# The last four products of a diffusion block's second MLP, and the final norm, in parts of 384 and 128 tokens instead of 256 and 256

## The reference

```python
def rms_norm(x, g, eps=NORM_EPS):
    y = xf * lax.rsqrt(jnp.mean(xf * xf, axis=-1, keepdims=True) + eps)
    return (y * g.astype(jnp.float32)).astype(x.dtype)

def squared_relu_mlp(h, w_in, w_out):
    return jnp.square(jax.nn.relu(h @ w_in)) @ w_out
...
        xl = xl + ml[5] * squared_relu_mlp(modulate(xl, norm_mlp_g[i], ml[3], ml[4]), w_mlp_in[i], w_mlp_out[i])
...
    return rms_norm(xl, final_norm_g)
```

## Time and profile before

| | before |
|---|---|
| median of 3 runs | 1615.22 us (1614.89 to 1615.65) |
| the profiled execution's own time | 1615.17 us |
| its span in the trace | 1613.4 us |
| TensorE busy (matmuls) | 1593.0 us, 99% |
| TensorE weight loads | 1432.4 us, 89% |
| VectorE, ScalarE, GpSimd busy | 983.9, 517.4, 617.5 us |
| first matmul of the last four units | 1578.87 us |
| last store issued | 1611.12 us |

### The profile page before, as it was taken

The page is one execution under the profiler, slowest core; times in us unless marked ns, Lnnn a source line. Parts: engine busy times, 40 slices in busy tenths (PEclk is TensorE's granted clock), DMA queues, the critical chain, the costliest instruction groups (busy, mean ns, idle before and its releaser), DMA issues.

```text
span 1613.4 us, 24201 instructions
## 1 busy us (share of the span) xinstructions
PE 1593.0 (99%) x9427; PEld 1432.4 (89%) x9427; DVE 983.9 (61%) x1316; ACT 517.4 (32%) x931; POOL 617.5 (38%) x402
## 2 busy tenths in 40 slices
PE   8999999999999999999999999999999999999997
PEld 5889988989999999999999888878889888888887
DVE  5697457258756764864784678229975825344354
ACT  4422466333211211211211512138864422222222
POOL 2422565335323322432331444244504644444441
PEclk9999999999999999999999999999999999999999
DMA  9473212213252234223332122110002322323221
GB/s 357 185 278 140 92 41 100 92 66 105 76 186 79 78 120 141 98 97 117 105 111 98 66 91 92 66 56 1 1 1 89 105 95 92 104 91 100 95 79 53
DMA packets 50334, 162.99 MB, mean 101 GB/s; under 512 B 6336, under 2 KB 8768, under 8 KB 46656
## 3 DMA queue, kind: packets, MB, share of 16 engines
q1 hardware_dynamic: 50240, 161.68, 28.8%
HBM read 158.78 MB, written 2.10 MB: 100 GB/s over the span
## 4 chain that ended last, share of the span: by engine, by line
PE 93%; DVE 2%; DMA 2%; issue 1%; ACT 1%; SPq 0%; POOL 0%; POOLq 0%; DVEq 0%; ACTq 0%
PE ps L1713 27%; PE ps L1714 26%; PE ps L1715 26%; PE ps L2239 3%; PE ps L2201 2%; PE ps L2228 1%; PE ps L2106 1%; PE ps L2094 1%; PE ps L2134 1%; PE ps L1918 1%; DMA mod_big<-w_mod_dram 1%; DMA mod_late<-w_mod_dram 1%; DMA raw<-units_dram 1%; PE ps L2129 1%; DVE h L1315 0%
## 5 line engine op out<-in xcount | busy, mean ns | idle before, releaser
L625 POOL TENSOR_TENSOR w_lo<-raw,w_hi 128x1024 fp32r<-128x1024 f32 (+1 forms) x235 | 483.3, 2068 | 838.3 <-ACT w_hi L784 838.1
L1713 PE MATMUL ps<-h,w_hi 128*128 128x384 f32 (+2 forms) x1176 | 409.8, 348 | 1.8 <-DVE h L1315 1.4
L1714 PE MATMUL ps<-h,w_lo 128*128 128x384 f32 (+2 forms) x1176 | 407.6, 347 | 0.0
L1715 PE MATMUL ps<-h,w_hi 128*128 128x384 f32 (+2 forms) x1176 | 407.3, 346 | 0.0
L784 ACT ACTIVATE w_hi<-raw 128x1024 fp32r<-128x1024 f32 x187 | 197.8, 1058 | 373.5 <-PE ps L1715 366.0
L1713 PE MATMUL ps<-hid_lo,w_hi 128*128 128x384 f32 (+2 forms) x800 | 277.6, 347 | 0.0
L1714 PE MATMUL ps<-hid_hi,w_lo 128*128 128x384 f32 (+2 forms) x800 | 276.5, 346 | 0.0
L1715 PE MATMUL ps<-hid_hi,w_hi 128*128 128x384 f32 (+2 forms) x800 | 276.4, 346 | 0.0
L1713 PEld LDWEIGHTS ps<-h,w_hi 128*128 128x128 f32 x1176 | 221.3, 188 | 25.3 <-issue 3.4
L1715 PEld LDWEIGHTS ps<-h,w_hi 128*128 128x128 f32 x1176 | 221.2, 188 | 16.4
L1714 PEld LDWEIGHTS ps<-h,w_lo 128*128 128x128 f32 x1176 | 221.3, 188 | 16.0
(11 more groups left out here) (233 smaller groups left out, 2264.5 us busy)
## 6 DMA issues: line engine op xcount, KB each, us to landing
raw<-units_dram SPq DMA_DIRECT2D x187, 512.0 KB, 3.3
mod_ring<-w_mod_dram SPq DMA_DIRECT2D x96, 256.0 KB, 3.3
mod_big<-w_mod_dram SPq DMA_DIRECT2D x16, 1024.0 KB, 10.6
mod_late<-w_mod_dram SPq DMA_DIRECT2D x8, 1024.0 KB, 8.0
xl<-x_dram SPq DMA_DIRECT2D x2, 2048.0 KB, 8.4
bias<-bias_dram SPq DMA_DIRECT2D x8, 384.0 KB, 3.8
xc<-ctx_dram SPq DMA_DIRECT2D x2, 1024.0 KB, 10.4
out_dram<-out_t SPq DMA_DIRECT2D x16, 128.0 KB, 1.9
```

The source lines that it names most:

```text
L625: ins = nc.gpsimd.tensor_tensor(w_lo[:, s, sl], raw[:, s, sl], w_hi[:, s, sl].bitcast(F32), op=ALU.subtract)
L1713: mm(out, a[0], b[1], start=start, stop=False)
L1714: mm(out, a[1], b[0], start=False, stop=False)
L1715: return mm(out, a[0], b[0], start=False, stop=stop)
```

## The change

The final norm and the four units ahead of it (i = 4) are cut at token 384 instead of 256; the norm behind the second attention (i = 3) is still cut at 256. All that follows from a part's width follows: additions, squares, sums, diagonals, spreads, results and stores.

```diff
-        rows_last = at("rows_last", [P, 256], F32, a_at)
-        x_gain = at("x_gain", [P, 3, 256], F32, a_at + size(256))
+        rows_last = at("rows_last", [P, P], F32, a_at)
+        x_gain = at("x_gain", [P, 3, P], F32, a_at + size(256))
...
+        LAST = 384
...
-            half = slice(256 * j, 256 * j + 256)
+            edge = 256 if i == 3 else LAST
+            half = slice(edge, LAT) if j else slice(0, edge)
             return xl, 0, half, half
...
-                sp.dma_start(t["out"][:, k, 0:256], out_t[:, k, 0:256]).then_inc(out_stored, 16)
+                sp.dma_start(t["out"][:, k, 0:LAST], out_t[:, k, 0:LAST]).then_inc(out_stored, 16)
...
-                sp.dma_start(t["out"][:, k, 256:LAT], out_t[:, k, 256:LAT]).then_inc(out_stored, 16)
+                sp.dma_start(t["out"][:, k, LAST:LAT], out_t[:, k, LAST:LAT]).then_inc(out_stored, 16)
...
-                nc.gpsimd.tensor_tensor(out_t[:, k, 256:LAT], x_gain[:, k - 5], rows_last[:], op=ALU.mult).then_inc(out_pool, 1)
+                nc.gpsimd.tensor_tensor(out_t[:, k, LAST:LAT], x_gain[:, k - 5], rows_last[:], op=ALU.mult).then_inc(out_pool, 1)
...
-                        nc.scalar.activation(x_gain[:, m - 5], xl[:, m, 256:LAT], ACT.Copy,
+                        nc.scalar.activation(x_gain[:, m - 5], xl[:, m, LAST:LAT], ACT.Copy,
                                              scale=gains[:, 4, m:m + 1]).then_inc(gain_made, 1)
...
-                nc.scalar.activation(rows_last[:], ps[:, 7, 0:256], ACT.Copy).then_inc(rows_copied, 1)
+                nc.scalar.activation(rows_last[:], ps[:, 7, 0:P], ACT.Copy).then_inc(rows_copied, 1)
```

## The result

The changed kernel takes 1618.18 us (median of 17 runs, 1617.3 to 1619.89) against 1615.08 us for the kernel before in the same sets of runs: 3.1 us more, a ratio of 1.0020 with a 95% interval of 1.0014 to 1.0027. The forecast was 1618.8.

What follows compares the result with a forecast made beforehand. TensorE's stream was taken as the bound until 1602.9, then a 10.4 us tail. TensorE +4.72 (5.13 - 0.79 - 0.05 + 0.22 + 0.21) less 1.15 gave +3.6 us: 1618.8 us, range 1617.6 to 1620.1.

Steps and rivals of the forecast that it cites:

- The first pass's term: First pass of the last four units: 96 matmuls go from 256 to 384 columns, 119.9 to 173.3 ns each, +5.13 us.
- The second pass: Last four units: 96 matmuls go from 256 to 128 columns, 119.9 to 111.7 ns each, bound by weight loads, -0.79 us.
- The doubt about the repeated column: The 111.7 ns came from matmuls whose stationary operand repeats one column; full MLP tiles might load more slowly, staying at 119.9 ns.
- The rival in which the loads hide: Second pass runs at 60 ns a step with weight loads hidden: 4.96 us less, 1613.8 us, not slower; chance 4%.
- one pair of starts at a seam: Starts at 1197.64 and 1197.70, behind a 512-wide matmul: taken to show 128 columns alone need about 60 ns.
- VectorE's cover: Last units' second pass: VectorE free after about 2.6 us, next unit ready after 2.68; under 0.1 us spare, costed at 0.
- Sums and spread in the stream: On TensorE between units: a third sum matmul, +0.22 us, and a spread of 384 columns instead of 256, +0.21 us.
- The tail: Behind the last addition: narrower work brings the first store 1.08 us earlier, landing may give 0.1; about 1.15 us back.
- The landing: Landing of the last stores, 1.7 to 1.9 us: 64 KB instead of 128 may give -0.1 us.
- The steps on SyncE's queue: Seven further steps between the last eight stores, 3.30 us, some 0.48 each, set by the queue; taken to stay.
- the rival of faster stores: Half the bytes let SyncE's queue issue every 0.39 us: tail gives 0.57 us more, 1618.2 us; chance 17%.

## Why the prediction was right

*What bounds the kernel.* TensorE's stream from the first matmul of the last four units to the last addition grew by 4.76 us where 4.72 were summed, and the kernel by 3.4 in the trace. The first pass's term, +5.13, was measured alone as +5.1, with steps of 173.3 ns.

*The second pass.* 111.4 ns a step against 111.7 taken from another part of the kernel. The doubt about the repeated column in those rows was unneeded: full tiles load as fast. The rival in which the loads hide fell twice, in the changed profile and in the run with half the weights: a hidden load cannot shorten the step when it is halved, and this one did, to 60.0 ns. That run turned the argument from one pair of starts at a seam into a measurement. The argument itself had misread the pair: in the kernel before, too, the second narrow matmul's load starts with the first narrow matmul (both at 1197.64), so "about 60 ns" for the columns alone was an upper bound. Nothing in the sum hangs on it.

The price of this rival was wrong, 4.96 us less for 96 shorter steps. It left out VectorE's cover, which the prediction had itself found thin. In the run with steps of 60.0 ns VectorE held units 6 and 7, and the kernel gained 2.5; by that run the rival would have come to about 1615.7 (an estimate), not 1613.8.

The Trainium skill, "TensorE: Matmul & The Clock Gate", section Back-to-back issue gap, gives columns / 2.4 + 2.5 ns for an isolated matmul, and says itself that at few columns this leaves the weight load out. So the 111.4 ns measured here, where it has 55.8, do not contradict that section; the rule is not meant for such a stream.

*Sums and spread in the stream.* From the last matmul ahead of the sums (1597.95) to the second one behind them (1598.85) are 0.90 us, 0.68 above two plain steps, against 0.45 before (1593.14 to 1593.83): +0.23, with +0.22 summed. The spread's two sides are alike: 1601.31 to 1602.17, 0.64 above two steps against 0.44 before (1596.46 to 1597.14), +0.20 for a summed +0.21.

*VectorE's cover* was put at under 0.1 us. It held, and was wider. The three wide results of unit 6's turn in the changed kernel:

```profile
1605.88 1.66 DVE L1379 SCALAR_TENSOR_TENSOR out_t<-xl,gains,ps 128x384 f32<-128x384 f32 x3
```

They end at 1607.54, and the addition of unit 7 starts at 1607.62, 0.31 us behind the start of the unit's last matmul, as before (0.32): TensorE released it. The 0.08 between them is not the whole cover, since in the run with half the weight loads, where VectorE had no gap, the addition starts 0.09 ahead of the recorded end of the results. VectorE's period there was 2.50 us, against TensorE's 2.68, so the cover was some 0.18.

*The tail* gave 1.26 us where the terms add to 1.18 (the prediction wrote "about 1.15"). Two of its sizes were off, in opposite directions, so part of this closeness is luck. The final spread was summed as 0.49 and took 0.80 at a clock of 0.50, which made the first store 0.13 later than forecast. The landing was taken as 0.1 shorter; it went from 1.9 to 1.6 us, and the end followed 0.25 sooner; 1.6 us stayed with half the bytes. The steps on SyncE's queue stayed, as the sum took them and as two queues confirmed, so the rival of faster stores did not hold.

*The verdict.* The forecast of 3.6 us stands against 3.4 in the profiled pair and 3.1 between medians. The 0.3 between the last two is the profiled executions' own place among their runs, 0.41 above the median in the changed kernel and 0.09 in the one before. The prediction drew a line at 1618.45, 0.2% above before, and gave 0.72 to a time above it. The median of 1618.18 lies just below, on the side that had 0.25. But 0.2% was too coarse for what could be told: with 17 runs of each kernel the interval is 0.14% to 0.27%, and the changed kernel is slower.

## What to carry to other kernels

In this kernel a stream of matmuls that each load 128 new weight columns has a floor of one weight load a step, 111.4 ns. Splitting tokens unevenly across that floor costs on the wide side what the narrow side cannot give back, here 45 ns for each pair. So in such a stream keep both parts above the width at which the load is covered (here 256, whose 119.9 ns are just over the 111.4; widths between 128 and 256 were not tried), and look for a shorter tail elsewhere. When a tail is cut, write down what is late next and how late: here a faster spread was worth nothing because the results ahead, and then the store queue, were already level with it.

## What had not been expected of the hardware

The granted clock fell at different distances behind the last unit's last matmul. Windows of the kernel before, then one of the changed kernel:

```profile
1606.40:1606.80 0.40, 0.38 (x2) 0.00 (x0) 0.40 (x2) 0.00 (x0) 0.00 (x0) 0.99 0.00 0
1606.80:1607.20 0.40, 0.00 (x0) 0.00 (x0) 0.01 (x1) 0.38 (x1) 0.00 (x0) 0.50 0.00 0
...
1609.20:1609.60 0.40, 0.00 (x0) 0.00 (x0) 0.16 (x1) 0.18 (x1) 0.00 (x0) 0.55 0.00 0
```

In the kernel before it fell at about 1606.8, 3.9 us behind the end of that matmul (1602.92) and with the end of the final spread. In the changed kernel a mean of 0.55 puts the fall at about 1609.24, 1.65 us behind (1607.59), although TensorE had made the final sums in between (1608.69 to 1609.07). The changed kernel with two queues did the same, 1.75 us behind, and its final spread lasted 0.80 us as well. But with half the weight loads the clock was 1.00 until 1607.98, 5.2 us behind and past the final spread (0.49 us). With the narrow second pass on the kernel before it fell at 1604.54, 3.8 us behind and only in the last 0.1 us of the spread, which lasted 0.70 as before. So it is not the narrow pass alone; what decides was not tried. The final spread of 128 columns, recorded as two, lasts 0.49 us at the full clock and 0.80 at half.
